# The last 512 columns of an expert's first weight chunk as sixteen eight-partition transfers

## The reference

```python
def expert_choice_ffn(h, w_router, w_gate, w_up, w_down):
    ...
    probs = jax.nn.softmax(t.astype(jnp.float32) @ w_router.astype(jnp.float32), axis=-1)
    aff, idx = lax.top_k(probs.T, cap)
    xe = t[idx]
    hid = jax.nn.silu(jnp.einsum("ecd,edf->ecf", xe, w_gate)) * jnp.einsum("ecd,edf->ecf", xe, w_up)
    ye = jnp.einsum("ecf,efd->ecd", hid, w_down) * aff[..., None].astype(h.dtype)
    out = jnp.zeros_like(t).at[idx.reshape(-1)].add(ye.reshape(-1, d))
```

## Time and profile before

| | |
|---|---|
| time, median of 3 runs (lowest to highest) | 2408.66 us (2408.6 to 2409.93) |
| the profiled execution: its time | 2407.7 us |
| its span, first to last instruction | 2405.8 us |
| granted TensorE clock, mean | 0.996 |
| PE busy | 2370.5 us, 99% |
| DVE, ACT, POOL busy | 1077.1, 519.3, 302.5 us |
| moved by DMA | 707.02 MB, mean 294 GB/s |

### The profile page before, as it was taken

One profiled execution on the slowest core, in us unless ns is written; L12 is line 12 of the kernel. 1 busy time (PEld: TensorE's weight loads), 2 busy tenths in 40 slices (PEclk: granted clock), 3 DMA queues, 4 the chain that ended last, 5 costly groups with the idle time before them and its releaser, 6 DMA issues.

```text
span 2405.8 us, 49544 instructions
## 1 busy us (share of the span) xinstructions
PE 2370.5 (99%) x21931; PEld 1625.6 (68%) x21931; DVE 1077.1 (45%) x2059; ACT 519.3 (22%) x1076; POOL 302.5 (13%) x417
## 2 busy tenths in 40 slices
PE   9999999999999999999999999999999999999997
PEld 8888999899898888745655455555555555444454
DVE  7989888888987634451221222122122112212213
ACT  6445444544534412200000000000000000000001
POOL 0422431341341000000000000000000000000001
PEclk9999999999999999999999999999999999999998
DMA  5233234223336545799999999999999999999996
GB/s 187 74 110 123 92 99 134 90 92 118 114 117 212 208 140 207 289 395 410 418 411 420 416 409 420 408 417 409 418 417 408 419 416 409 420 406 416 420 409 259
DMA packets 88646, 707.02 MB, mean 294 GB/s; under 512 B 11824, under 2 KB 16048, under 8 KB 51568
## 3 DMA queue, kind: packets, MB, share of 16 engines
q1 hardware_dynamic: 65504, 628.96, 64.4%
q0 software_dynamic: 14368, 56.80, 7.5%
q10 hardware_dynamic: 8560, 18.10, 2.0%
HBM read 669.76 MB, written 34.06 MB: 293 GB/s over the span
## 4 chain that ended last, share of the span: by engine, by line
PE 47%; DMA 10%; DVE 0%; issue 0%; POOL 0%; POOLq 0%; SPq 0%; ACT 0%; DVEq 0%
PE p_gu L2653 31%; PE p_y L2671 8%; DMA raw<-in_w_e 7%; PE p_y L2674 4%; PE p_z L2674 2%; DMA raw_first<-in_w_e 2%; DMA raw<-xa 1%; PE p_gu L1592 1%; DVE raw L2587 0%; DMA out<-raw 0%; DVE xg L2579 0%; POOLq L2725 0%; POOL out L2489 0%; PE off_banks L1606 0%; SPq L2421 0%
## 5 line engine op out<-in xcount | busy, mean ns | idle before, releaser
L2653 PE MATMUL p_gu<-raw,xT 128*32 128x512 f32 (+1 forms) x8160 | 888.6, 556 | 2.3 <-DMA raw<-in_w_e 2.2
L2653 PEld LDWEIGHTS p_gu<-raw,xT 128*32 128x32 f32 x8160 | 393.8, 110 | 362.8 <-issue 231.0
L2538 DVE SCALAR_TENSOR_TENSOR tg<-tg,p_gu 128x256 f32<-128x256 f32 (+1 forms) x144 | 57.4, 399 | 1051.6 <-ACT tg L2501 1047.1
L2671 PE MATMUL p_y<-raw,hidT 128*32 128x384 f32 x3744 | 433.3, 486 | 0.0
L1282 PE MATMUL pp<-h,wx_hi 128*128 128x256 f32 (+1 forms) x1664 | 423.9, 346 | 0.5 <-ACT fo L836 0.5
L2501 ACT ACTIVATE tg<-p_gu 128x256 f32<-128x256 f32 (+1 forms) x144 | 52.8, 367 | 1266.6 <-PE p_gu L2653 1249.0
L2674 PE MATMUL p_y<-raw,hidT 128*32 128x256 f32 x1248 | 319.5, 379 | 0.0
L1282 PEld LDWEIGHTS pp<-h,wx_hi 128*128 128x128 f32 x1664 | 282.9, 190 | 31.0 <-ACT fo L836 0.7
L1282 PE MATMUL pp<-h,wx_lo 128*128 128x256 f32 (+1 forms) x832 | 281.3, 338 | 0.0
L2674 PEld LDWEIGHTS p_y<-raw,hidT 128*32 128x32 f32 x1248 | 137.2, 110 | 100.1 <-issue 32.1
L2674 PE MATMUL p_z<-raw,hidT 128*32 128x256 f32 x624 | 184.8, 379 | 0.0
(11 more groups left out here) (297 smaller groups left out, 2951.1 us busy)
## 6 DMA issues: line engine op xcount, KB each, us to landing
raw<-in_w_e SPq DMA_DIRECT2D x185, 2048.0 KB, 32.0
raw<-in_w_e SPq DMA_DIRECT2D x58, 1536.0 KB, 32.5
raw_first<-in_w_e SPq DMA_DIRECT2D x23, 2048.0 KB, 33.3
w_raw<-in_w_x SPq DMA_DIRECT2D x48, 512.0 KB, 3.5
dec<-acs POOLq DMA_DIRECT2D x48, 512.0 KB, 4.8
raw<-in_w_e SPq DMA_DIRECT2D x16, 1024.0 KB, 32.6
w_raw<-in_w_g SPq DMA_DIRECT2D x24, 512.0 KB, 3.4
g_tab<-gx POOLq DMA_DIRECT2D x8, 1152.0 KB, 6.0
```

The source lines that it names most:

```text
L2538: dve.scalar_tensor_tensor(out=tg[:, r % 2, 0:w], in0=tg[:, r % 2, 0:w], scalar=1.0, in1=p[:, 0:w], op0=ALU.add, op1=ALU.mult).then_inc(s_ ...
L2653: mm = pe.matmul(p_gu[g][quad(q), 0:w], xT[:, e % 2, k * SLOTS + 32 * g:k * SLOTS + 32 * (g + 1)], slot[:, at:at + w], start=(k == 0), sto ...
L2671: pe.matmul(y_first[half][quad(g), :], hidden(g), w[:, half * 3 * P:(half + 1) * 3 * P], start=first, stop=last)
```

## The change

In the first gate and up chunk of each expert (i = 0 of its first block, a chunk of 4096 columns), the last 512 columns are left out of the chunk's transfer. They come in sixteen transfers of eight partitions behind it: for r = 0 to 3 and q = 0 to 3 the partitions 32q + r, 32q + r + 4, ... , 32q + r + 28. Expert 0 is left as it is (its chunk is one of the first ten, `c >= RAW`), so 15 chunks are changed. All seventeen transfers count on the slot's semaphore, 16 each, and PE waits for as many.

```diff
+LOW_COLS = 512
+EIGHTS = [slice(32 * q + r, 32 * (q + 1), 4) for r in range(4) for q in range(4)]
+
+
+def in_pieces(c):
+
+    kind, b, i = chunk(c)
+    return c >= RAW and kind == "gu" and i == 0 and b % NB == 0
+
+
+def landings(c):
+
+    return sum(16 * (1 + len(EIGHTS)) if in_pieces(n) else 16 for n in range(c % RAW, c + 1, RAW))
+
+
@@ load_part
     src = A["w_e"][e:e + 1, at * P:(at + w) * P].rearrange("e (p n) -> p (e n)", p=P)
-    sp.dma_start(raw[c % RAW][:, 0:w], src).then_inc(s_raw[c % RAW], 16)
+    own = w - (LOW_COLS if in_pieces(c) else 0)
+    sp.dma_start(raw[c % RAW][:, 0:own], src[:, 0:own]).then_inc(s_raw[c % RAW], 16)
+    if own < w:
+        for rows in EIGHTS:
+            sp.dma_start(raw[c % RAW][rows, own:w], src[rows, own:w]).then_inc(s_raw[c % RAW], 16)
@@ loaded
                 c = CHUNK_OF[kind, b, i]
-                pe.wait_ge(s_raw[c % RAW], (XT_LOADED if c % RAW < EARLY_RAW else 0) + 16 * (c // RAW + 1))
+                pe.wait_ge(s_raw[c % RAW], (XT_LOADED if c % RAW < EARLY_RAW else 0) + landings(c))
                 return raw[c % RAW]
```

## The result

The changed kernel takes 2445.45 us (median of 5 runs, 2444.27 to 2446.83) where the kernel before took 2409.09 us beside it: a ratio of 1.015, 95% interval 1.0137 to 1.0164. It is 36 us slower, where 2402.5 us were forecast, with 0.17 for slower. The profiled execution has a span of 2444.0 us. One execution among all that follow, of the kernel with eight loads in a burst, took 3994.58 us at a granted clock of 0.571 and is left out of that kernel's time.

What follows compares the result with a forecast made beforehand. The prediction took PE and DMA as almost in balance, with late engines setting PE's waits. Stall -4.8 and tail -1.4 make -6.2 us: 2407.7 becomes 2401.5, plus 0.96 for the median gives 2402.5 us; range 2400 to 2410.5.

Steps and rivals of the forecast that it cites:

- What bounds the kernel: Expert stage: PE and DMA almost in balance, DMA needing about 1% more per expert; PE loses 4.8 us waiting for weights.
- instruction fetches: Expert stage: possible source of the late engines' lag, 125 us on queue 8, or 16 us each on eight engines alone.
- the price of the pieces: Changed chunks: pieces cost their eight engines 16 x 0.09 = 1.45 us more, 0.58 less, so +0.87 us a chunk.
- the bet on which engines are late: Pieces use engines 0 to 7; if the other eight are late, their relief brings the 20 us lead to -2: balance.
- Late and leading halves: Stage's end: DMA share 0.51 read as eight engines running, eight dry; lead about 20 us, 1.45 us per expert.
- The wrong eight: Rival: pieces land on the engines already late, whose +13 us come out one to one: 2422; chance 0.10.
- SP: SP's queue: 16 more issues of 0.33 us, 5.3 us per changed chunk, covered by the backlog of 32.6 us.
- Price of a row saved: Main transfer of changed chunks: rows 0.073 us shorter, eight per engine, 0.58 us saved per chunk on every engine.
- The tail: Kernel's end: `xa` lands 7 to 8 us earlier, so the second half's sum follows PE at once: 1.4 us gained.
- No relief: Rival: pieces stay on their partitions' usual engines, or writes into partitions another engine fills slow it: 2408.7; chance 0.17.
- The window: Rival: SP's limit on transfers under way is filled by 16 pieces, engines run dry, +70 us: 2479; chance 0.07.
- Its second reading: SP's limit counts rows per engine (nine per chunk, two per piece): pieces fill a third, nothing runs dry.

Runs made afterwards that it cites:

- the kernel with eight loads in a burst: Kernel before plus eight unread loads of eight partitions (256 B rows) in a burst behind each of 15 chunks: 2424.39 us.
- pieces of four rows: Changed kernel with sixteen pieces of four partitions (0 to 63 only), the other 64 partitions in one transfer: 2442.29 us.
- one-row loads: Kernel before plus 240 unread loads of one partition, one 256 B row, one behind each of sixteen chunks per expert: 2408.61 us.
- the loads apart: Kernel before plus 240 unread eight-partition loads of 256 B rows, one behind each of sixteen chunks in a row per expert: 2416.43 us.
- the burst: Kernel before plus 240 unread eight-partition loads of 256 B rows, sixteen together behind one chunk per expert: 2448.32 us.
- The 6 us hold: Changed kernel with the 512 columns as one 128-partition transfer, SP held by 200 already met waits behind each cut chunk: 2410.36 us.
- The one-transfer kernel: Changed kernel with the 512 columns as one transfer of 128 partitions instead of sixteen of eight: 2410.2 us, ratio 1.0008.
- the full burst: Kernel before plus sixteen unread loads of 128 partitions with 32 B rows in a burst behind each of 15 chunks: 2462.66 us.

## Why the prediction was wrong

**What bounds the kernel** was right. PE and DMA are in balance, the late engines alone set PE's waits, and 2388.5 + 14 r, made from the prediction's own 1.45 us per expert and 4.8 us, gives r to within 0.4 us an expert of what the traces' rhythm shows. The 1.45 itself, read from the lag of half of the engines, comes back in the rhythm of the kernel before: 86.7 - 85.17 = 1.5 us an expert. (It is 1.7% of 85.17, not the "about 1%" of the prediction.) That instruction fetches are what makes eight engines late was not tested.

**The step that failed first is the price of the pieces**, "16 x 0.09 = 1.45 us". It took a row's price from stretches in which many rows of one transfer follow each other (0.0365 us per KB and 0.013 fixed) and gave it to transfers that have one row on an engine. Measured, sixteen such transfers in a row cost their engine 3.2 us, 0.2 each. The price per packet was not wrong (0.034 us each for 256 B rows apart); what was missing is the time between transfers, which no row of the trace before could show, and for which the range should have had a bound.

**The second is the bet on which engines are late**, "If the relieved ones are the late ones". Eight rows do go to eight engines: SP's queue has 69344 - 65504 = 3840 packets more, 15 x 16 x (8 + 8). That agrees with the Trainium skill (DMA: Bandwidth & Descriptors, Why a DMA increments its semaphore by 16 and not by 1). That they are the lowest-numbered is that section's alone, since the traces name no engines. The same section says that the issuing engine itself adds the rest of the sixteen at once, and the trace agrees: each piece has nine landing events, the first at its issue. But the late eight aren't the other half. Two of them are among the eight that carry the pieces, and two among the four that carry pieces of four rows: the same two, if the four are part of the eight. Neither is the engine that carries one-row loads. Late and leading halves, 20 us apart, were read from a share of 0.51; that says how many are late, not which.

By the sum: with the predicted 1.45 us per chunk, and two late engines hit, r = 1.45 + 0.87 = 2.32 and 2421 us, what the rival *The wrong eight* gave (2422). The other 24 us are the bursts. And with the pair not hit, a leading engine with no lag of its own and 3.20 - 0.58 = 2.62 us per expert would still give 2388.5 + 14 x 2.62 = 2425 us. Either failed step alone was enough to lose the gain.

**SP**: "16 more issues of 0.33 us" are 0.62 us each at the least, 10 us per cut chunk, and more where SP is held. That they are covered was right in effect: the loads apart have as many issues an expert, and as long, and in the burst no weight chunk lands sooner than 19.2 us after its issue. The 6 us hold agrees.

**Price of a row saved**: 0.58 us per cut chunk was not measured by itself. The one-transfer kernel, which saves and pays it back, is at 1.0008.

**The tail**: nothing of the 1.4 us. `xa` now lands 25.8 to 29.0 us after its issues at 2392.8 to 2399.8, brought by the late pair, and the second half's sum stands where the earlier trace rows had it, behind the norms:

```profile
2426.63 0.61 DVE L2594 SCALAR_TENSOR_TENSOR xg<-p_y,aff,xg 96x384 f32<-96x384 f32 x1
...
2428.28 0.61 DVE L2594 SCALAR_TENSOR_TENSOR xg<-p_y,aff,xg 96x384 f32<-96x384 f32 x1
```

**The rivals.** *No relief* was wrong about the mechanism: it is not the bytes. *The wrong eight* was right in sign and for two of eight engines; its 0.10 was too little for what is one of many ways in which two sets of eight can lie. *The window* cost nothing that shows in the changed kernel: SP is held for up to 9.7 us at an issue, but the slowest engine never runs dry. Its second reading (entries per engine) is the one that the full burst supports. The rule that warned of small transfers (the Trainium skill, DMA: Bandwidth & Descriptors, Rules for kernel authors) was set aside by the earlier trace rows, in which small rows, not small transfers, keep the engines full. Its sign was right. The prediction's 2 us for each are not in that section; the page has them in Anatomy of one DMA — SWDGE (gpsimd) path, as the fixed time of a transfer that GpSimd issues. One after the other they are wrong here: 0.2 us on the engines that carry it, and 0.03 where the small transfers stand alone.

**No version beats the kernel before.** The most that any relief of the late engines could bring is the stall of 4.8 us and the 1.4 of the tail. The one-row loads fit the lead of one engine only; its 20 us, shared by the fifteen others, are 20 / 16 = 1.3 us, an estimate below what can be measured. That kernel wasn't tried.

## What to carry to other kernels

Price a DMA by transfers per engine, not by packets and bytes: in a queue that is full, a small transfer that stands alone costs about its packets, but in a row of more than three or four each further one costs its engines up to 0.2 us. If small ones can't be avoided, put large ones between them. And a share of 0.5 at the end of a stage says how many engines are late; before work is moved between engines, find which they are, with a small unread load whose engines are known.

## What the runs showed of the hardware

- Small transfers that follow each other in SP's queue land every 0.18 to 0.2 us on an engine, at 256 B and at 2 KB, while their packets take 0.03 to 0.1 us. The Trainium skill (DMA: Bandwidth & Descriptors, Queues, rings and completion order) says that a completion is written only after all earlier writes of its engine have landed; a fixed wait of that kind for each transfer would look like this. No run here separates it from other reasons.
- An issue of SP takes 0.33 us at the least for 128 partitions and 0.62 us for eight partitions four apart. That of a one-row load takes 0.29 us.
- What SP may have under way is not a fixed number of transfers. With two entries for each on an engine more than twenty were under way; with nine entries each and 32 B rows SP was held up to 13 us and its queue ran nearly empty.
- In the kernel with bursts of unread loads five waits of PE for a weight chunk (one of 3.7 us, four of 2.0 us) were followed by 3.4 us at the 1.2 GHz level. The same 48 matmuls took 6.93 us there and 5.33 at the full clock.
